# An encoder layer on one core: another order of VectorE's steps in the retention part, and y's squares in four sums

## The reference

```python
h = _rmsnorm(x, g_mix) * (1.0 + scale1) + shift1
q, k, v, g_sw, p, gate_a, gate_b = jnp.split(h @ w_in, IN_SPLITS, axis=-1)
qh, kh = _rotary(q), _rotary(k) * RET_QK_DIM ** -0.5          # 8 heads of 64, v of 128
ret = retention(qh, kh, vh, forwards) + retention(qh, kh, vh, backwards)
#   per chunk of 128 tokens: inner = (q k^T * decay_in) v ; cross = (q * decay_q) state
#   state = decay_chunk * state + (k * decay_k)^T v
ret = (ret - mean(ret)) * rsqrt(var(ret) + EPS) * ret_gn_gain
branch_a = silu(g_sw) * ret
pooled = window_mean(p, 2 | 4 | 8 | 16) - p
branch_b = (pooled @ w_pool_grp) * pool_scale
merged = sigmoid(gate_a) * branch_a + sigmoid(gate_b) * branch_b
x = x + gate1 * (merged @ w_out)
h2 = _rmsnorm(x, g_ffn) * (1.0 + scale2) + shift2
x = x + gate2 * (gated_conv_mlp(h2))
y = _rmsnorm(x, g_final)
```

## Time and profile before

| | us |
|---|---|
| median of 3 runs | 2655.47 (2651.19 to 2658.2) |
| the profiled execution | 2655.73 |
| its span, first to last instruction | 2653.9 |
| PE busy | 2544.1 |
| DVE / POOL / ACT busy | 1844.2 / 1721.6 / 1148.2 |
| mean granted clock of PE | 0.979 |

### The profile page before, as it was taken

The page is one execution under the profiler, slowest core; times in us unless marked ns, Lnnn a source line. Parts: engine busy times, 40 slices in busy tenths (PEclk is TensorE's granted clock), DMA queues, the critical chain, the costliest instruction groups (busy, mean ns, idle before and its releaser), DMA issues.

```text
span 2653.9 us, 34758 instructions
## 1 busy us (share of the span) xinstructions
PE 2544.1 (96%) x12660; PEld 2128.9 (80%) x12660; DVE 1844.2 (69%) x2246; ACT 1148.2 (43%) x1738; POOL 1721.6 (65%) x1184
## 2 busy tenths in 40 slices
PE   6999999989999999999989999999999999999998
PEld 3788888977778888878867888889787788888886
DVE  4878797966786666665858787879668655556434
ACT  5332323325555454555624323232356555555443
POOL 1565766886377777655656658677573877775545
PEclk9999999999999999999999999999999999999998
DMA  8114232346234555497631322313351333325664
GB/s 322 40 66 136 77 124 84 122 159 229 61 127 147 167 167 166 154 343 230 189 110 41 129 84 97 116 66 116 123 182 31 105 119 104 98 97 176 214 194 146
DMA packets 296008, 362.14 MB, mean 136 GB/s; under 512 B 17312, under 2 KB 178464, under 8 KB 295840
## 3 DMA queue, kind: packets, MB, share of 16 engines
q1 hardware_dynamic: 292960, 349.44, 40.4%
q10 hardware_dynamic: 2880, 10.49, 1.1%
HBM read 284.36 MB, written 75.50 MB: 136 GB/s over the span
## 4 chain that ended last, share of the span: by engine, by line
PE 79%; DVE 10%; issue 3%; ACT 3%; POOL 3%; DMA 2%; SPq 1%; DVEq 0%; POOLq 0%; ACTq 0%
PE ps L1094 26%; PE ps L1260 14%; PE ps L1518 12%; PE ps L1450 9%; PE ps L1155 5%; PE ps L1469 2%; PE ps L1359 2%; DVE state L2861 2%; PE ps L1537 1%; PE ps L1562 1%; PE ps L1563 1%; PE ps L1192 1%; PE ps L1572 1%; DVE qdT L2842 1%; PE ps L1303 1%
## 5 line engine op out<-in xcount | busy, mean ns | idle before, releaser
L2216 POOL TENSOR_TENSOR f_w<-f_ring,f_w 128x512 fp32r<-128x512 f32 x434 | 596.6, 1381 | 396.7 <-ACT f_w L1805 391.3
L1094 PE MATMUL ps<-hc_hi,f_w 128*128 128x512 f32 x2240 | 690.5, 389 | 3.5 <-ACT u_act L1879 2.8
L2155 POOL TENSOR_TENSOR f_w<-f_ring,f_w 128x512 fp32r<-128x512 f32 x282 | 460.8, 1641 | 336.9 <-ACT f_w L1639 336.3
L1094 PEld LDWEIGHTS ps<-hc_hi,f_w 128*128 128x128 f32 x2240 | 419.9, 188 | 93.2 <-ACT u_act L1879 3.6
L1094 PE MATMUL ps<-hc_lo,f_w 128*128 128x512 f32 x1120 | 435.7, 389 | 0.0
L1260 PE MATMUL ps<-act_ring,f_w 128*128 128x512 f32 x1848 | 422.6, 391 | 2.3 <-DVE act_ring L2537 2.3
L1260 PEld LDWEIGHTS ps<-act_ring,f_w 128*128 128x128 f32 x1848 | 347.9, 188 | 75.9 <-issue 3.7
L1805 ACT ACTIVATE f_w<-f_ring 128x512 fp32r<-128x512 f32 x434 | 269.8, 623 | 249.9 <-POOL f_ring L2226 109.4
L1518 PE MATMUL ps<-hb,f_w 128*128 128x512 f32 x1440 | 355.3, 401 | 6.9 <-ACT swish L1675 5.8
L1639 ACT ACTIVATE f_w<-f_ring 128x512 fp32r<-128x512 f32 x282 | 176.6, 628 | 373.8 <-PE ps L1518 148.3
L1518 PEld LDWEIGHTS ps<-hb,f_w 128*128 128x128 f32 x1440 | 273.2, 192 | 71.4 <-issue 7.7
(11 more groups left out here) (263 smaller groups left out, 4065.1 us busy)
## 6 DMA issues: line engine op xcount, KB each, us to landing
f_ring<-in_w_in SPq DMA_DIRECT2D x176, 256.0 KB, 4.0
f_ring<-in_w_up SPq DMA_DIRECT2D x160, 256.0 KB, 3.4
f_ring<-gated_out SPq DMA_DIRECT2D x154, 256.0 KB, 3.0
late_rows<-in_w_late SPq DMA_DIRECT2D x64, 512.0 KB, 5.4
gated_out<-gated_up SPq DMA_DIRECT2D x44, 512.0 KB, 4.1
f_ring<-down_sums SPq DMA_DIRECT2D x88, 256.0 KB, 3.0
gated_out<-t_gated SPq DMA_DIRECT2D x22, 768.0 KB, 6.3
f_ring<-in_w_down SPq DMA_DIRECT2D x66, 256.0 KB, 3.6
```

The source lines that it names most:

```text
L1094: ins = pe.matmul(ps_row[:, half_of(bank)], a[:, cols], b, start=i in (0, 1, 3) and k == 0 and n == 0, stop=k == KQ - 1 and n == 2, skip_g ...
L2155: pool.tensor_tensor(out[:, 1, :], raw, out[:, 0, :].bitcast(F32), ALU.subtract).then_inc(mix_lo.sem, 1)
L2216: pool.tensor_tensor(piece_slot(q)[:, 1, :], piece_raw(q), piece_slot(q)[:, 0, :].bitcast(F32), ALU.subtract).then_inc(piece_lo.sem, 1)
```

## The change

Seven edits. (1) DVE's order in pairs 1 to 3: scores(0) directly behind decayed_q(0), two pool levels and scores(1) next, the last two levels behind states(0). (2) In all pairs, states(1), swish(1) and decayed_q(1) stand ahead of the moments of head 0 (`statistics(0)`, `aggregate(0)`), with an explicit wait for O0. (3) In pair 0 decayed_k(0) goes behind t_piece_low(3), and pool levels and means go ahead of sums and scores; ACT makes t_piece_high(2) four steps earlier. (4) Late tiles: pair 0 takes four instead of two, pair 3 four instead of six; `late(3)` is now behind normed(0), `late(4)` where `late(5)` was, `late(5)` between the last two sums. On SP the loads for `late(5)` go between the sixth and seventh weight load of the next pair. (5) POOL's root for head 0 one piece later. (6) At the swap, POOL makes six low halves ahead of the first root instead of three, and for half 1 four sums instead of seven; PE sums 16 columns instead of four over them. (7) PE does the statistics and the spread of half 0 six steps earlier.

```diff
--- before.py
+++ after.py
@@ -73,7 +73,7 @@
 ADA_SLOT = 0
 LATE_TILES = 4 * D // P
 LATE_RING = 2
-LATE_AT = ((0, 0, 0, 0, 0, 2), (2, 2, 2, 2, 2, 2), (2, 2, 2, 2, 2, 2), (2, 2, 2, 0, 0, 0))
+LATE_AT = ((0, 0, 0, 0, 2, 2), (2, 2, 2, 2, 2, 2), (2, 2, 2, 2, 2, 2), (2, 2, 0, 0, 0, 0))
 OUT_UNIT_AT = (("set", 0, 3), ("set", 1, 0), ("set", 1, 4), ("set", 2, 1))
 
 
@@ -461,7 +461,7 @@
         hf_done = tally("h_full_done", 0, first=KC + 4, swap=KC + 2)
         hlo_done = tally("h_lo_done", 0, first=KC + 4, swap=KC + 2)
         y_squared = tally("y_squared", 0, swap=2 * KC, last=2 * KC)
-        y_low = tally("y_sum_low", 0, swap=14, last=10)
+        y_low = tally("y_sum_low", 0, swap=11, last=10)
         y_gained = tally("y_times_gain", 0, last=4)
         y_low_scaled = tally("y_scaled_by_pool", 0, last=4)
         y_stat = tally("y_stat_summed", 0, swap=2, last=2)
@@ -978,11 +978,14 @@
                         late_load(seq, late[0])
                         late[0] += 1
 
-                late_loads(0, 5)
+                late_loads(0, 4)
                 for pr in range(1, PAIRS):
                     where = ("mix", seq, pr)
                     with_units = seq == 0 and pr == PAIRS - 1
-                    for j in range(KC):
+                    for j in range(KC - 2):
+                        mix_in(where, j)
+                    late_loads(pr - 1, 5)
+                    for j in range(KC - 2, KC):
                         mix_in(where, j)
                     late_loads(pr, 0)
                     sp.wait_ge(*filled(("mix", seq, pr - 1), "BB1"))
@@ -1006,8 +1009,6 @@
                         out_unit_store(0)
                         out_unit_load(1)
                     late_loads(pr, 4)
-                    if pr < PAIRS - 1:
-                        late_loads(pr, 5)
                     if with_units:
                         for u in range(1, PAIRS - 1):
                             out_unit_store(u)
@@ -1274,18 +1275,24 @@
             def statistics_of_y(where, half):
 
                 at_end = half == 1 and where[0] == "last"
-                slots = (0, 4, 5, 6, 7) if at_end else (0,)
+                slots = (0, 4, 5, 6, 7) if at_end else (0, 2, 4, 6) if half else (0,)
                 if at_end:
                     pe.wait_ge(*y_row_done.at(where, 1))
-                for n in slots:
-                    if n:
-                        pe.wait_ge(*squared(where, half, n))
-                    else:
-                        pe.wait_ge(*low_sums(where, half, 3 if len(slots) > 1 else 7))
-                    for t in range(4):
-                        col = (4 + t) * HALF + 4 if at_end else Y_STAT_BANK[where[0]] * HALF + 4 * half + t
-                        ins = pe.matmul(ps_row[:, col:col + 1], y_sq[where[1]][half][:, n, t * P:(t + 1) * P], ones[:, 0:1],
-                                        start=n == 0, stop=n == slots[-1])
+                def column(n, t):
+
+                    col = (4 + t) * HALF + 4 if at_end else Y_STAT_BANK[where[0]] * HALF + 4 * half + t
+                    return pe.matmul(ps_row[:, col:col + 1], y_sq[where[1]][half][:, n, t * P:(t + 1) * P], ones[:, 0:1],
+                                     start=n == 0, stop=n == slots[-1])
+
+                if at_end:
+                    for n in slots:
+                        pe.wait_ge(*(squared(where, half, n) if n else low_sums(where, half, 3)))
+                        for t in range(4):
+                            ins = column(n, t)
+                else:
+                    pe.wait_ge(*low_sums(where, half, 4 if half else 7))
+                    for t, n in itertools.product(range(4), slots):
+                        ins = column(n, t)
                 ins.then_inc(y_stat.sem, 1)
 
             def spread_y(where, half):
@@ -1391,9 +1398,9 @@
 
                     if n == 8:
                         pe.wait_ge(*x_updated.at(("ffn", 0, 0), 4 * PRODUCTS))
-                    if n == 16:
+                    if n == 10:
                         statistics_of_y(pre, 0)
-                    if n == 21:
+                    if n == 15:
                         spread_y(pre, 0)
                     if n == 26:
                         statistics_of_y(pre, 1)
@@ -1985,11 +1992,11 @@
                         copy_v(pair, 0)
                         piece_after(pair, 5)
                         copy_v(pair, 1)
+                        t_piece_high(pair, 2)
                         piece_after(pair, 6)
                         copy_v(pair, 2)
                         copy_v(pair, 3)
                         piece_after(pair, 7)
-                        t_piece_high(pair, 2)
                     else:
                         for q in range(2 * PRODUCTS):
                             if q in (1, 3, 5, 13):
@@ -2277,19 +2284,17 @@
             for seq in range(N_SEQ):
                 if seq:
                     swap = ("swap", 0, 0)
-                    for q in range(3):
+                    for q in range(6):
                         mix_low(("mix", 1, 0), q)
                     rstd_of_y(swap, 0)
-                    for q in range(3, 6):
-                        mix_low(("mix", 1, 0), q)
-                    squares_of_y(swap, 1, Y_SUMS)
+                    squares_of_y(swap, 1, ((0, 0, 1), (0, 2, 3), (0, 4, 5), (0, 6, 7)))
                     rstd_of_y(swap, 1)
                 for pr in range(PAIRS):
                     pair = ("mix", seq, pr)
                     for q in range((6 if seq else 4) if pr == 0 else 0, MIX_PIECES[pr]):
                         at_q = mix_kind(pr, q)
                         mix_low(pair, q)
-                        if at_q in (("set", 1, 5), ("set", 2, 3)):
+                        if at_q in (("set", 1, 6), ("set", 2, 3)):
                             h = at_q[1] - 1
                             pool.wait_ge(*veps_done.at(pair, h + 1))
                             inverse_root(grs[:, :], veps[:, :]).then_inc(grs_done.sem, 1)
@@ -3015,24 +3020,24 @@
                         rope_sums(2)
                         rope_sums(3)
                         t_piece_low(2)
-                        decayed_k(0)
                         pool_pads()
                         t_piece_low(3)
+                        decayed_k(0)
                         pool_level(0)
                         queries()
                         decayed_k(1)
                         decayed_q(0)
                         pool_level(1)
+                        pool_level(2)
                         unit_add(0, 0)
                         scores(0)
+                        pool_level(3)
                         unit_add(0, 1)
-                        pool_level(2)
+                        pool_means()
                         unit_add(0, 2)
                         scores(1)
                         first_states(0)
                         states(0)
-                        pool_level(3)
-                        pool_means()
                     else:
                         late(0)
                         qkv_add(0)
@@ -3047,41 +3052,41 @@
                         queries()
                         decayed_k(1)
                         decayed_q(0)
-                        late(3)
+                        scores(0)
                         add_p()
                         pool_level(0)
-                        scores(0)
-                        for level in range(1, 3):
-                            pool_level(level)
+                        pool_level(1)
                         scores(1)
                         first_states(0)
                         states(0)
+                        pool_level(2)
+                        pool_level(3)
                         unit_add(0, 0)
-                        pool_level(3)
+                        pool_means()
                         unit_add(0, 1)
-                        pool_means()
                         unit_add(0, 2)
                     swish(0)
+                    dve.wait_ge(*filled(where, "O0"))
+                    first_states(1)
+                    states(1)
+                    swish(1)
+                    decayed_q(1)
                     statistics(0)
                     aggregate(0)
-                    swish(1)
-                    first_states(1)
-                    states(1)
-                    decayed_q(1)
                     unit_add(1, 0)
                     centred(0, None)
                     normed(0)
+                    late(3)
+                    unit_add(1, 1)
                     if pr == 0:
                         silu_of_rows(seq)
-                    unit_add(1, 1)
-                    late(4)
                     unit_add(1, 2)
                     statistics(1)
                     aggregate(1)
                     gate_a(0)
                     centred(1, "TR0")
                     branch_a(0)
-                    late(5)
+                    late(4)
                     if pr == PAIRS - 1:
                         late_part(seq)
```

(1 more changed line is left out.)

## The result

The changed kernel takes 2628.26 us (median of 4 runs, 2627.2 to 2632.94) where the kernel before takes 2654.3 on the same chip: a ratio of 0.9905, with an interval of 0.9886 to 0.9923. So the sign was right and the size was not: 26 us were gained where 74.5 were forecast, and 2628 lies outside the range of 2565 to 2613.

What follows compares the result with a forecast made beforehand. PE, busy 2544.1 of 2653.9 us, sets the time, so removing its idle or slow-clock time pays. Gains 41.6 + 13.7 + 3.2 + 4 + 12 = 74.5 us from 2655.7 give 2581.2, range 2565 to 2613.

Steps and rivals of the forecast that it cites:

- The prices of the stalls in the middle pairs: Pairs 1 and 2: stalls at products(0), 7.7 us, and outputs(1), 3.9, go; 11.6 us for each of four pairs.
- rival (2): outputs(1) held by ACT's tanh or GpSimd, not DVE's order, so stalls there stay: 33 us less gain, 2614; chance 0.07.
- Pair 3: Fewer late tiles ahead of scores: gain 3.2 us in sequence 1 and 4 us (2 to 8) in sequence 0.
- a period over 132 us: Sign of a wrong forecast: pairs 1 and 2 from one qkv start to the next, expected 129.6 instead of 140.0.
- The transitions: Six passages into pairs 1, 2, 3: late last tiles make a new PE stall, 1.2 us each (0 to 3).
- rival (3): Slower than before: DVE stands at late(5) for a load behind weight loads, delaying the next pair; 2681 at 22 us landing; chance 0.05.
- the bound of 3 us for a stall: Upper end of the new PE stall at each of the six passages into the next pair, taken as 1.2 us.
- Pair 0: Old stalls of 14.1 and 9.6 us go, 5 us charged in each sequence for new ones: gain 13.7 us.
- the line of durations from 101.5 to 115.7: DVE's work ahead of scores(0) in pair 0, ending after PE asks at 113.4: new stall of about 2 us.
- Rival (1): DVE and GpSimd get in each other's way more once PE no longer pauses: 45 us lost, 2626; chance 0.12.
- The swap: Four GpSimd sums, 16 PE columns (+2.4 us), earlier statistics: 48.4 us laid out for 60.9, gain taken as 12 (9 to 12.4).
- the bad end of the sum: All terms at their bad bounds: 34.4 + 8 + 1.4 + 2 + 9 = 55 us gained, 2601.

Runs made afterwards that it cites:

- loads_first: Changed kernel with SP's two loads for a pair's last late tiles back ahead of all the next pair's weight loads: 2627.45 us.
- v_sum_first: Changed kernel with DVE's two late(1) tiles put behind the v sum instead of before it, in pairs 1 to 3: 2602.32 us.
- late5_back: Changed kernel with late(4) put back ahead of sum (1, 5), late(5) ahead of normed(1), and late(5)'s loads ahead of the next pair's weight loads: 2622.39 us.
- p0_pool_held: Changed kernel with one wait added: in pair 0 GpSimd holds its set 1 weight sums until DVE has done scores(0): 2621.83 us.
- all_three: Changed kernel with v sum ahead of late(1), pair 0's pool levels behind states(0), and seven sums, four columns and later statistics at the swap: 2582.4 us.
- swap_seven: Changed kernel with the swap's second statistics as before: seven GpSimd sums and four PE columns instead of four and sixteen: 2628.14 us.

## Why the prediction was wrong, and where it was right

**Right.** The prices of the stalls in the middle pairs: 44.6 us for the 46.4 of the sum, and 7.2 for 7.7 in the run with scores(0) alone. That a stall costs more than its idle time is seen in pair 2 of sequence 0: the clock is 0.50 behind the 4.82 idle us, and a product group takes 3.75 us there for 1.78. outputs(1) no longer wait, by ACT and GpSimd neither, so rival (2) is out. Pair 3 gained 3.5 and 4.8 us for 5.2 (the 4 of the sum and its transition) and 4.4, with GpSimd still waiting at the out units.

**The signs.** The prediction called a period over 132 us wrong for pairs 1 and 2, where it expected 129.6. In sequence 0 they last 135.8 and 133.7 us: the units came out as laid out, and the qkv parts did not.

**The transitions, the largest error: 33.8 us for 7.2.** The mechanism was named (rival (3) had it too) and the size was wrong in three steps. First, the landing: I took the median, 5.4 us, for loads that go out together with eight weight loads; it was 7.8, above the longest of the earlier trace rows, and the last sum ended at +3.6 us, not +0.5. Second, the bound of 3 us for a stall was too low by my own rows: the landing of 7.6 and two long tiles give a last sum at -9.5 + 7.6 + 4.6 + 0.6 = +3.3, 5.3 later than before, and so a stall of 4. (The +1.3 given for the end of the tiles is not from these terms either: with the median landing and two long tiles it is +0.5, with the longest landing +2.7.) Third, the slow group behind a stall (1.6 us here) was counted for the stalls that go and not for the ones that come. Behind this is the step that no better landing time would have mended: I asked how late DVE would be and not what it has to do until PE needs it. loads_first shows that the DMA wait, though real, isn't the cause, and v_sum_first, where the wait stays and the stall goes, shows it again: DVE's chain from branch_b(0) to the v sum takes 33 to 35 us of 34.7, so whatever stands at the end of a pair, a wait or two tiles, comes out as a stall. late5_back (the tiles away from the end of the pair) and v_sum_first (two others away from the chain) shorten it at either end, and both bring the qkv parts back.

**Pair 0: 13.7 us forecast, 0.3 lost.** The failed step is the line of durations from 101.5 to 115.7. The order was laid out rightly, but with short forms (1.3 for a level, 2.4 for decayed_q(0)) at a place where GpSimd has no pause. scores(0) ended at 120.4, and the stall was 6.65 us, not 2. With the old stalls gone (3.6 and 4.2 us) and the new ones come, the sum is zero. Rival (1) is right here: contention is 2.8 and 3.9 us of the two stalls by p0_pool_held, and about 2 and 1 more by the long forms left in that run, which leaves about the 2 us that the prediction had for the order. For the whole kernel it is right in part. DVE is busy for 1866.0 us where it was for 1844.2, with the same 2246 instructions, so on the whole they did get slower; scaling the normed result (10.9 us more), the pool levels behind the first (10.3) and decayed_q (7.1) lead. But the middle pairs did not lose by it, and not all operations got slower. The median of the 64 late tiles was 2279 ns; in the changed kernel it is 1524 (ns min/median/max):

```profile
L2647 DVE SCALAR_TENSOR_TENSOR late_rows<-late_rows,silu_row x64: 1211/1524/2316, 164.1 to 1790.0; 128x1024 f32<-128x1024 f32 x64
```

Whether two instructions meet is a matter of place, and changed with each move here (1366 in v_sum_first). How much of the transitions' loss is contention wasn't tried: a run that holds GpSimd there holds the weights that PE needs next.

**The swap: 7.3 us for 12.** The 2.4 us for twelve more columns were 3.0, and the slow stretch behind them (7.22 us for 4.36) wasn't in the sum. That explains 3.5 of the 4.7 missing; the rest I did not take apart. The failed step is the price of the columns, 0.2 us each and no effect on the clock. The layout of 48.4 us was short by about 2 us besides: all_three, with four columns, a wait of 0.51 us and no slow stretch, takes 48.65 us where it gives 48.4 - 2.4 + 0.5 = 46.5.

**The chances.** 0.12 for rival (1), at 2626, is nearest to the result, but for another reason than it gave, and the range left it out. That it is near is luck, as its 34 us of stalls in the pairs did not come. A bound of 4 to 5 us instead of 3 on the transitions would not have been enough: with the 5.6 that they took, the bad end of the sum is about 2617, and with nothing from pair 0 instead of 8 us about 2625.

## What to carry to other kernels

When work is moved past a boundary, lay out the engine's whole chain up to the next point where another engine asks for it, and compare its length with the time that there is. A wait in that chain which the trace names need not be the cause: with a chain that fills its time, removing the wait only makes room for the next thing in it, and shortening the chain at its end is what helps. Give a DVE operation its short duration only where GpSimd is idle beside it (a pool level took 1.3 us with GpSimd's sums held and 2.2 us beside them), and count for each new stall the slow stretch behind it as well, as for each one that goes (7.51 us for 5.92 behind 3.08 us of idle time).

## What the runs showed of the hardware

With one-column matmuls (fp32, 128 x 128 against 128 x 1) in a row at the swap, PE's granted clock went from 1.00 to 0.50 while PE was busy without a gap. Behind or within sixteen of them it fell in all eight profiles that have them there: within them in the changed kernel (0.50 from 1352.7 on), just behind them in v_sum_first (1.00 until 1338.70, 0.50 from 1340.00 to 1342.00). Within 32 it fell in the one profile there is (1.00 until 1349.00, 0.50 from 1351.00 on). Behind four of them at the swap it stayed at 1.00, after 0.51 us of idle time (all_three) and after 2.50 us (swap_seven). A busy share of 100% was thus no sign that the clock would hold: in these windows it does not follow the busy share that the profile's rows show. What sets it was not shown.
